# Blocks of 32 slots on four column groups, 4 KB runs for the down matrices, a gather in every block, three weight buffers

## The reference

```python
lg = hf @ w_rg + b_rg;  grp = argmax(lg)              # top-1 of 8 groups
le = (hf @ w_re + b_re).reshape(N, 8, 8)[grp]          # experts of that group
top_v, top_j = lax.top_k(le, 2)                        # 2 of its 8 experts
wts = softmax(lg)[grp] * softmax(top_v)
eid = grp * 8 + top_j                                  # 1024 (token, choice) pairs over 64 experts
y   = (silu(x @ w_g[e]) * (x @ w_u[e])) @ w_d[e]       # w_g, w_u: 1024x512, w_d: 512x1024, fp32
out[token] += wts * y
```

```
[25 11 15 29 12 25 28 23] [ 6 20 26 45  0 17 27 21] [ 8 14 11 22 11 10 10 14] [ 1  0  4  4  3  0  2  0]
[10  4  4  6  4  3  4 15] [16 43  6 20  0  6  9  8] [18  7 10  9 11  5  5  5] [44 26 11 70 71 66 24 40]
```

## Time and profile before

| | |
|---|---|
| median of 3 executions | 1318.48 us |
| span of the profiled execution | 1317.8 us (the page gives no other time for it) |
| PE, PEld busy | 1145.9 us (87%), 559.4 us (42%) |
| DVE, ACT, POOL busy | 364.1, 234.4, 227.7 us |
| moved by DMA | 417.15 MB, mean 317 GB/s |
| chain that ended last | PE 45%, DMA 42% (of it the up matrices 40%), DVE 6% |
| costliest group | gate and up products, L1775: 1984 rows, 461.1 us |

### The profile page before, as it was taken

One profiled execution on the slowest core, in us unless ns is written; L12 is line 12 of the kernel. 1 busy time (PEld: TensorE's weight loads), 2 busy tenths in 40 slices (PEclk: granted clock), 3 DMA queues, 4 the chain that ended last, 5 costly groups with the idle time before them and its releaser, 6 DMA issues.

```text
span 1317.8 us, 15984 instructions
## 1 busy us (share of the span) xinstructions
PE 1145.9 (87%) x5149; PEld 559.4 (42%) x5150; DVE 364.1 (28%) x720; ACT 234.4 (18%) x496; POOL 227.7 (17%) x271
## 2 busy tenths in 40 slices
PE   6999999999999999999888898877788777887881
PEld 5788776778853333333322222222222222222220
DVE  3899334354355222222210101001000010000005
ACT  4232324573110000000010111001100011000012
POOL 3455444083000000010001011000010000100010
PEclk9999999999999999999999999999999999999996
DMA  6431211234069999999999889999999999999684
GB/s 227 125 126 64 97 70 61 98 122 192 19 261 377 362 412 419 418 414 423 384 427 425 352 365 428 432 430 429 427 431 430 429 428 430 427 423 422 283 379 194
DMA packets 56837, 417.15 MB, mean 317 GB/s; under 512 B 10384, under 2 KB 10541, under 8 KB 26090
## 3 DMA queue, kind: packets, MB, share of 16 engines
q1 hardware_dynamic: 51354, 411.45, 75.4%
q0 software_dynamic: 5312, 5.28, 1.2%
q10 hardware_dynamic: 144, 0.07, 0.0%
HBM read 410.45 MB, written 18.36 MB: 325 GB/s over the span
## 4 chain that ended last, share of the span: by engine, by line
PE 45%; DMA 42%; DVE 6%; ACT 3%; issue 2%; SPq 1%; POOL 0%; DVEq 0%; POOLq 0%; ACTq 0%
DMA sb_weights<-in_w_exp_up 40%; PE ps_proj L1775 13%; PE ps_proj L1492 10%; PE ps_scores L1795 6%; PE ps_proj L1722 4%; PE ps_proj L1543 2%; DVE ps_scores L1015 1%; PE ps_proj L1670 1%; PE ps_proj L1674 1%; PE ps_proj L1667 1%; PE ps_proj L1622 1%; PE ps_proj L1625 1%; PE ps_proj L1628 1%; PE ps_aT L1784 1%; DMA sb_weights<-in_w_exp_gate 1%
## 5 line engine op out<-in xcount | busy, mean ns | idle before, releaser
L1775 PE MATMUL ps_proj<-sb_weights,sb_scratch 128*64 128x512 f32 x1984 | 461.1, 616 | 52.1 <-DMA sb_weights<-in_w_exp_up 49.7
L1775 PEld LDWEIGHTS ps_proj<-sb_weights,sb_scratch 128*64 128x64 f32 x1984 | 159.9, 141 | 344.3 <-issue 341.7
L1795 PE MATMUL ps_scores<-sb_weights,sb_scratch 128*64 128x512 f32 x992 | 228.5, 597 | 21.8 <-ACT sb_scratch L938 21.8
L1376 DVE TENSOR_TENSOR sb_scratch<-sb_scratch,ps_proj 128x256 f32<-128x256 f32 x62 | 26.1, 421 | 549.0 <-ACT sb_scratch L936 549.0
L695 POOL TENSOR_TENSOR sb_tick<-sb_tick 1x1 f32<-1x1 f32 x62 | 11.5, 185 | 851.5 <-ACT sb_scratch L943 851.5
L1795 PEld LDWEIGHTS ps_scores<-sb_weights,sb_scratch 128*64 128x64 f32 x992 | 67.0, 136 | 145.6 <-issue 109.5
L1492 PE MATMUL ps_proj<-sb_hT_r,sb_ring_r 128*128 128x512 f32 x512 | 123.9, 394 | 0.0
L936 ACT ACTIVATE sb_scratch<-ps_proj 128x256 f32<-128x256 f32 x62 | 23.8, 384 | 495.9 <-PE ps_proj L1775 495.9
L1492 PEld LDWEIGHTS ps_proj<-sb_hT_r,sb_ring_r 128*128 128x128 f32 x512 | 94.8, 188 | 26.7 <-issue 6.5
L640 POOL TENSOR_TENSOR sb_ring_r<-sb_ring,sb_ring_r 128x1024 fp32r<-128x1024 f32 x32 | 76.2, 2392 | 65.0 <-ACT sb_ring_r L755 64.0
L943 ACT ACTIVATE sb_scratch<-ps_scores 128x512 f32 (+1 forms) x62 | 37.0, 597 | 269.1 <-PE ps_scores L1795 269.1
(11 more groups left out here) (314 smaller groups left out, 879.6 us busy)
## 6 DMA issues: line engine op xcount, KB each, us to landing
sb_weights<-in_w_exp_up SPq DMA_DIRECT2D x59, 2048.0 KB, 14.7
sb_weights<-in_w_exp_down SPq DMA_DIRECT2D x59, 2048.0 KB, 10.4
sb_weights<-in_w_exp_gate SPq DMA_DIRECT2D x59, 2048.0 KB, 22.1
sb_ring<-in_w_in SPq DMA_DIRECT2D x9, 2048.0 KB, 8.7
sb_x<-in_x SPq DMA_DIRECT2D x8, 512.0 KB, 5.1
sb_dense<-expert_rows SPq DMA_DIRECT2D x4, 1024.0 KB, 8.1
sb_ring<-in_w_conv_pw SPq DMA_DIRECT2D x1, 2048.0 KB, 9.0
sb_ring<-in_w_attn_up SPq DMA_DIRECT2D x1, 2048.0 KB, 7.7
```

Of the source, the lines that this page charges most:

```text
L1376: dve.tensor_tensor(act, gsig, ps_gu[:, 256:512], ALU.mult).then_inc(act_ready, 1)
L1775: last = mm(ps_gu[g * BLK:(g + 1) * BLK, :].rearrange("p (a n) -> p a n", a=2), hTb[:, c, half * BLK:(half + 1) * BLK], weights[:, slice(6 ...
L1795: last = mm(ps_y[g * BLK:(g + 1) * BLK, :], actT[:, j, half * BLK:(half + 1) * BLK], weights[:, place(parity, 4 + half), 2 * j + g, :], st ...
```

## The change

- Blocks have 32 slots (`BLK = 32`, `NG = 4`). The stationary operands are 32 columns wide, and each product runs on one of four column groups with 256 moving columns; four groups side by side take neighbouring quarters of the output.
- Every block is gathered, in the block before it; the sorted store and the copies from it are gone. The copies of gathered and of transposed rows go from DVE to ACT.
- There are three weight buffers (`NBUF = 3`): the third lies over `scratch` and `work`. Small working tiles move into a new tile `late`.
- Down matrices are read in runs of 4 KB.
- Experts are ordered by their place in the group, descending, over the groups, and fall into three classes, one for each buffer. Position p = 3r + c belongs to class c. An expert keeps its buffer for all its blocks. Classes with fewer blocks get idle turns after their first expert; an idle position does all the work of a position, on empty slots. The first five in the order always get a block and a load.
- Static loads are of the first three experts; the down matrix of the third waits for `slots_done`. Load n waits for the position three before the one at which its expert starts.
- The scattered rows have 256 values, 128 rows a position; `release` is gone, ACT and DVE wait for the scatter of three positions before.

The diff, cut to its core:

```diff
-BLK = 64
-AHEAD = 2
+BLK = 32
+NG = P // BLK
+NBUF = 3
+FIRST = 5
+MAXPOS = 162
...
+    pos, order = np.arange(MAXPOS), NE - 1 - np.arange(NE)[:, None]
+    cls = order % NBUF
+    put("turn", np.where(pos[None] % NBUF == cls, pos[None] // NBUF, -1))
+    put("class_before", (cls == cls.T) & (order < order.T))
+    put("expert", number % GROUPS * EPG + number // GROUPS)
+    put("always", order < FIRST)
+    put("movable", order >= NBUF)
...
-            wd = ap("w_exp_down")[0].rearrange("e (h p j) n -> e p h (j n)", h=2, p=P)
+            wd = ap("w_exp_down")[0].rearrange("e (k p) n -> e p k n", p=P)
...
-            for i in range(3):
-                load_third(0, i, zero, in_w)
-            load_third(1, 0, one, in_w1)
+            load_first(0, 0)
+            load_first(1, 1)
+            load_first(1, 2)
+            load_first(1, 0)
+            load_first(2, 1)
+            sp.wait_ge(logits_done, 1)
+            load_first(2, 0)
             sp.wait_ge(listed, 1)
             sp.dma_start(g_fin[:, :], ...)
+            def load_gate_up(n, e, base, free):
+                sp.wait_ge(in_w[0], 16 * n)
+                sp.wait_ge(gu_done, free)
+                sp.sem_inc(place_free, 1)
+                load_third(base, 0, e)
+                sp.wait_ge(in_w[1], 16 * n)
+                load_third(base, 1, e)
+            def load_down(n, e, base, free):
+                sp.wait_ge(down_done, free)
+                sp.wait_ge(in_w[2], 16 * n)
+                load_third(base, 2, e)
+            values = load_values(NBUF)
+            load_gate_up(NBUF, *values)
+            sp.wait_ge(slots_done, 1)
+            load_first(2, 2)
+            load_down(NBUF, *values)
+            n_loads = sp.value_load(loads_i, min_val=FIRST, max_val=NE)
+            with sp.Fori(NBUF + 1, n_loads) as n:
+                values = load_values(n)
+                load_gate_up(n, *values)
+                load_down(n, *values)
...
+            def position(p, c, r):                      # ACT
+                act_e.wait_ge(gu_done, p + 1)
+                act_e.activation(gsig, ps_gu[:, 0:P], ACT.Silu).then_inc(gsig_ready, 1)
+                copy_rows(p + 1)
+                act_e.wait_ge(actT_done, p + 1)
+                act_e.activation(actT, ps_actT[:, 0:P], ACT.Copy).then_inc(actT_ready, 1)
+                rows_to_block(p + 1)
+                act_e.wait_ge(down_done, p + 1)
+                if not isinstance(r, int):
+                    act_e.wait_ge(y_out[c], 16 * r)
+                act_e.activation(y_sb[c], ps_y[:, 0:QCOLS], ACT.Copy).then_inc(y_ready, 1)
...
+                link(dve.tensor_tensor(eblk, eblk, const("always", NE), ALU.max))
+                link(dve.tensor_scalar(own_turns, own_turns, -1.0, rounds, ALU.mult, ALU.add))
+                link(dve.tensor_scalar(turn_lo, own_turns, const("movable", NE), ps_tables[0:NE, 8:9], ALU.mult, ALU.add))
+                link(dve.tensor_scalar(first_pos, turn_lo, float(NBUF), const("class", NE), ALU.mult, ALU.add))
+                link(dve.tensor_scalar(free_after, first_pos, float(1 - NBUF), None, ALU.add))
...
+            static_onehot(0); count_blocks(); static_onehot(1); static_onehot(2); place_turns()   # DVE, in this order
+            gate_and_up(0); list_loads(); take_loads(); place_rows(); gate_and_up(1)
+            next_onehot(0, 0); prepare_slots(); gate_and_up(2); next_onehot(1, 1); take_slots()
...
+            def gather(p, c):
+                pe.wait_ge(hot_b, p + 1)
+                for t in range(T):
+                    for g in range(NG):
+                        last = mm(ps_rows[g * BLK:(g + 1) * BLK, 0:QCOLS], onehots[c][:, t, :],
+                                  h2[:, t, g * QCOLS:(g + 1) * QCOLS], start=t == 0, stop=t == T - 1)
+                last.then_inc(rows_done, 1)
+            def gate_up(p, c, loads):
+                pe.wait_ge(hTb_ready, p + 1)
+                pe.wait_ge(in_w[0], 16 * loads)
+                pe.wait_ge(in_w[1], 16 * loads)
+                for r in range(KD):
+                    rows = hTb[:, r % 2 * P + r // 2 * BLK:r % 2 * P + (r // 2 + 1) * BLK]
+                    at = 6 * c + r // 4
+                    for g in range(NG):
+                        cols = slice(g * P, (g + 1) * P)
+                        last = mm(ps_gu[g * BLK:(g + 1) * BLK, 0:2 * P].rearrange("p (a n) -> p a n", a=2),
+                                  rows, weights[:, at:at + 3:2, r % 4, cols], start=r == 0, stop=r == KD - 1)
+                last.then_inc(gu_done, 1)
+            def down(p, c, loads):                      # 4 x 4 products of 256 columns, wait on in_w[2]
...
+            gather(0, 0); transpose_rows(0); turns_of_classes(); gate_up(0, 0, 1); first_row(); gather(1, 1)   # PE
+            transpose_act(0); transpose_rows(1); load_rows(); down(0, 0, 1); gate_up(1, 1, 2); gather(2, 2)
+            transpose_act(1); transpose_rows(2); slot_rows(); down(1, 1, 2); gate_up(2, 2, 3); gather(3, 0)
+            transpose_act(2); transpose_rows(3); down(2, 2, 3)
...
+            with pe.Fori(1, n_rounds) as r:
+                for c in range(NBUF):
+                    p = NBUF * r + c
+                    loads = pe.value_load(loads_at[0:1, bass.ds(p, 1)], min_val=1, max_val=NE)
+                    gate_up(p, c, loads)
+                    gather(p + 1, (c + 1) % NBUF)
+                    transpose_act(p)
+                    transpose_rows(p + 1)
+                    down(p, c, loads)
```

More of the change, by code:

```diff
@@ L76 @@
 for _n, _w in [("ident", P), ("before", P), ("ones", P), ("pos", BLK), ("block", MAXPOS),
-               ("flip", P), ("lane8", EPG), ("row", 2 * T), ("half", 1), ("ahead", 1), ("ahead_slot", AHEAD), ("mask", P),
-               ("turn", MAXPOS), ("class_before", NE), ("nat_add", MAXPOS), ("load_add", MAXPOS), ("expert", 1),
-               ("first_pos", 1), ("number", 1), ("class", 2), ("bucket", 5 * P)]:
+               ("flip", P), ("lane8", EPG), ("row", 2 * T), ("quarter", 1), ("mask", P),
+               ("turn", MAXPOS), ("class_before", NE), ("class_of", NBUF), ("class", 1), ("base", 1), ("expert", 1),
+               ("always", 1), ("movable", 1), ("bucket", 5 * P)]:
     CONST[_n] = (_at, _w)
@@ new lines, in block_kernel @@
+        gbest, code, m1, m2, d_e, gden, eden = (late_temp(T) for _ in range(7))
+        ecount, eblk, used, unused, first_pos = (late_temp(1, rows=NE) for _ in range(5))
+        turn_lo, turn_hi, rounds, own_turns, load_no, load_next, free_after = (late_temp(1, rows=NE) for _ in range(7))
+        own_hot, ecmp = late_temp(NBUF, rows=NE), late_temp(SEQ // BLK, rows=NE)
+        first_of, rank_of, steps_of, pos_of, slot_of = (late_temp(2 * T) for _ in range(5))
+        steps = late_temp(2 * T, SEQ // BLK)
@@ L954, in _ @@
+            copy_rows(0)
+            rows_to_block(0)
+            for c in range(NBUF):
+                position(c, c, 0)
+            act_e.wait_ge(listed, 1)
+            n_rounds = act_e.value_load(rounds_i, min_val=2, max_val=ROUNDS)
+            with act_e.Fori(1, n_rounds) as r:
+                for c in range(NBUF):
+                    position(NBUF * r + c, c, r)
             for t in range(T):
@@ new lines, in transpose_act @@
+            def transpose_act(p):
+                pe.wait_ge(act_ready, p + 1)
+                pe.transpose(ps_actT[:, 0:P], act, ident).then_inc(actT_done, 1)
+            def down(p, c, loads):
+                pe.wait_ge(actT_ready, p + 1)
+                pe.wait_ge(in_w[2], 16 * loads)
+                for k in range(NG):
+                    for g in range(NG):
+                        last = mm(ps_y[g * BLK:(g + 1) * BLK, 0:QCOLS], actT[:, k * BLK:(k + 1) * BLK],
+                                  weights[:, 6 * c + 4 + k // 2, k % 2 * 2 + g // 2, g % 2 * QCOLS:(g % 2 + 1) * QCOLS],
+                                  start=k == 0, stop=k == NG - 1)
+                last.then_inc(down_done, 1)
@@ L1867, in _ @@
[L1867 to L1880 removed]
+            gather(0, 0)
@@ new lines, in _ @@
+            transpose_rows(0)
+            turns_of_classes()
+            gate_up(0, 0, 1)
+            first_row()
+            gather(1, 1)
+            transpose_act(0)
+            transpose_rows(1)
+            load_rows()
+            down(0, 0, 1)
+            gate_up(1, 1, 2)
+            gather(2, 2)
+            transpose_act(1)
+            transpose_rows(2)
+            slot_rows()
+            down(1, 1, 2)
+            gate_up(2, 2, 3)
+            gather(3, 0)
+            transpose_act(2)
```

738 lines of the change are left out of this document (250 added, 488 removed).

## The result

The changed kernel takes 1344.81 us (median of 4 runs, 1343.06 to 1345.21) against 1319.12 (1318.29 to 1320.92): ratio 1.0186, 95% interval 1.0171 to 1.02. Slower, as forecast, but by 25.7 us and not by 13. The profiled execution has a span of 1342.7 us where the sum said 1331.0, so the working has to be found short by 11.7 us.

The account below looks back on a forecast made before the run. Expert stage taken as DMA-bound for two thirds of its length. Stream start 360.8, stream 895.3, g_final 1.2, idle 37.9, landing to 1296.1, +3 +1.8 +27.8, products +2.3: span 1331.0, predicted 1332 us; range 1306 to 1370.

Parts of the forecast that it names:

- The extra load: Expert stage: an always-loaded expert without tokens makes 60 loads instead of 59, +15.1 us if the stream stays the limit.
- the shorter runs: Down matrices read in 4 KB runs: +0.15 us a load taken (bounds 0 to +0.18), +9 us over 60.
- Positions: PE's time for one position: 128 records at 56 ns plus 0.9, 8.1 us, under the DMA's 15.09 a load.
- rivals 2 and 3: Column groups overlap only partly, 1358 or about 1480, chance 0.15; PE's loop refetched every round, 1345 to 1375, chance 0.08.
- Rival 2: Four column groups on PE don't overlap fully: 80 ns a record, 1358 us; at 107 ns about 1480; chance 0.15.
- The last landing: End of the expert stage: 1277.05 us in the kernel before, forecast at 1296.1 in the changed one.
- the split against now: Difference to the kernel before: stream +25.0, idle -6.8, landing +0.9, end -10, clock +1.8, products +2.3, together +13.2 us.
- Rival 1: The third buffer pays: restart and stall at experts 60 and 61 shrink within 37.9 us of idle; 1306 us, chance 0.22.
- The stalls: DMA idle: 16.9 + 4 us at the start, 17 at experts 60 and 61, 37.9 together; slower products there +2.3.
- The stream: Weight loads in the expert stage: 178 of 180 thirds at 15.09 us a load, 895.3 us.
- The tail: After the last down products to the kernel's end: 28.0 us less 0.2 for a narrower copy, 27.8.
- The third buffer: Three weight buffers for two: gain nothing in the plain stretch, where the rate is the link's either way.

Follow-up runs that it names:

- hold_two: Changed kernel, but from the fifth load on each load waits one position longer, as with two buffers: 1375.31 us against 1344.81.
- split_16k: Changed kernel without the empty expert's load, idle turns last, down matrix in 16 KB runs, sixteen small products replacing the activations' transposition: 1298.51 us.

## Why the prediction was right, and what it missed

**Direction, and the two terms that made it.** The extra load cost 14.8 us (forecast 15.1) and the shorter runs 0.12 x 60 = 7 (forecast 9).

**Positions and rivals 2 and 3.** 7.99 us for 8.1, 54 ns a record for 56. Rival 2 is out. Here row and rule part: a record of 256 columns costs 223 ns on the whole array and 54 on a quarter, a speedup of 4.1; the Trainium skill (TensorE: Matmul & The Clock Gate, Measured speedup vs the span model) has 2.38 for three column tiles of 512 columns. The measurement decides.

**The last landing.** The prediction took the landing of the last up matrix, 1277.05, for the last landing of the kernel before. But the last down matrix of an expert is issued some 5 us behind the last up matrix and lands as much later: in that trace the last completion of the down third comes at 1281.94. The sum does not use this, but the split against now does. With the true landings, and 14.96 for the step of now, idle and landing together fell by 1.7 us (forecast 6.8 - 0.9) and the end with its tail by 3.8 (forecast 10 - 1.8). In the changed kernel the last completions are at 1305.40 (up) and 1310.63 (down):

```profile
1290.48 0.34 SPq L561 DMA_DIRECT2D sb_weights<-in_w_exp_up  x1
1295.80 0.39 SPq L564 DMA_DIRECT2D sb_weights<-in_w_exp_down  x1
```

**Rival 1.** The stalls did not shrink, they grew. The balance by the prediction's own terms: the last landing is at 1310.6; less 0.9 for landing, 1.2 for g_final, 360.8 and 178/3 x 15.20 = 901.9, leaves 45.8 us of idle, for 37.9 + 2.3 forecast. The restart came as walked: gate and up of position 2 were to end at 407.0, and the load that waits for them is issued at 407.42. What follows was not. Up matrices leave at 721.32 and 788.71 in SP's queue, three steps apart:

```profile
721.32 0.34 SPq L561 DMA_DIRECT2D sb_weights<-in_w_exp_up  x1
...
752.15 0.34 SPq L561 DMA_DIRECT2D sb_weights<-in_w_exp_up  x1
...
776.33 0.34 SPq L561 DMA_DIRECT2D sb_weights<-in_w_exp_up  x1
...
788.71 0.34 SPq L561 DMA_DIRECT2D sb_weights<-in_w_exp_up  x1
```

67.4 - 3 x 15.2 = 21.8 us lost at experts 60 and 61, for 17. From 788.71 to 1305.40 are 34 steps of 15.20, so nothing is lost behind it, and the other 24.0 us lie at the start, for 20.9. The windows above say the same: 37, 379 and 122 GB/s over 17, 17 and 9 us are 24 us of a stream at 421 lost. Of the 3.1 and 4.8 us over the forecast, 1.5 and 3.1 are PE coming out of a wait at a lower clock, which the sum had priced at the end alone. At the start the down products of position 2 take 3.20 us (425.71 to 428.91) for 1.7, in a window with a granted clock of 0.79, and the next down third leaves at 429.35 for 427.5. In the middle the first gate and up takes 6.60 us in the chain for 3.46 (granted clock 0.79 over 736 to 752):

```profile
721.32 15.27 DMA sb_weights<-in_w_exp_up
736.58 0.14 issue
736.72 6.60 PE ps_proj L1664 x64
```

**Where the 11.7 us are.**
- The stream, +6.6: the step is 15.20 for 15.09. I took the step of now from one pair of rows, 14.94, where the mean is 14.96; +0.15 for the runs was a little too much; and 0.12 comes with the new layout, of which the scatters of the stretch explain about 0.04 and neither the runs, nor PE's clock, nor the length of the scattered rows the rest. This term was mis-sized.
- The stalls, +5.6: 45.8 for 40.2, as above. This term was mis-sized too.
- From the last landing to the end of the last down, 0: 1310.6 to 1315.4 is 4.8 us, for 3 + 1.8. The picture was right: gate and up (1305.54 to 1310.67) run while the down third lands, and at the lower clock. In the window of the last 10 us the DMA still moves 0.35 MB:

```profile
1306.00:1316.00 10.00, 9.17 (x127) 5.47 (x119) 1.06 (x5) 1.60 (x5) 0.05 (x1) 0.83 0.09 35
```

- The tail, 27.3 for 27.8: -0.5.

So the direction rests on the two terms above and was no luck. The two mis-sized terms both made the kernel slower than forecast, and neither hid the other.

**The third buffer** was costed at nothing in the plain stretch, which hold_two bears out. What the prediction did not say is that with the third buffer held back this layout would have been 30 us slower still.

## What to carry to other kernels

When a kernel waits for its stream, count the transfers and walk through the restarts: here one needless load and the place of idle turns were worth 37 us, more than the whole change cost. Take a step from the mean of many, not from one pair of rows, and over a stretch with the same side traffic. Price the first products behind every wait at the lower clock, not only the last ones, and check which of several transfers in flight lands last. Lengthen the runs of a transfer by moving the permutation into a write of DVE and small products, not into a strided moving operand of the large ones.

## What the runs showed of the hardware

- A moving operand of fp32 with a stride of 16 bytes takes 113 ns for 256 columns on a column group, for 54 with neighbouring ones. The Trainium skill (SBUF — State Buffer, Door 1: The DMA port swizzle, the note on cachelines) says that lines of 16 bytes want at least two hits each for full bandwidth. By this rule the trace agrees: with a stride of 16 bytes each line is hit once, and the products take 2.1 times as long.
- Four column groups of 32 overlap: 54 ns a record of 256 columns, for 223 on the whole array. With products of 32 moving columns, 32 records take 0.49 us, 15 ns each (split_16k).
- A second scatter of up to 128 rows of 1 or 2 KB takes 0.31 to 0.37 us from the stream, for 0.15 and 0.11 by its bytes.
- A load is landed when the last of its 16 completions is in, and these drift apart under a steady stream: in the changed kernel the completions of a down third are spread over 0.8 us behind the stall in the middle and over 7.3 us at the end (1303.37 to 1310.63).
- The same load costs 15.20, 15.08 and 15.00 us with its down third in runs of 4, 8 and 16 KB.
- With 7 us of waits a load the granted clock was 0.84 over 900 to 1050 us. In the groups read here that start out of a wait the 64 records took 5.3 to 6.6 us; in the last of them (1305.54 to 1310.67) the granted clock was 0.50 over 1306 to 1308, which is 1.2 GHz, and 1.00 over 1310 to 1311. Filled waits brought 0.99 and 3.5 us, and nothing to the step of the stream (15.22 for 15.20).
